# Gated delta rule in a fused three-layer kernel: decays from one product, keys turned ahead of their stages

## The chip, the cores and the metric

The kernel runs on one core of a Trainium2 chip. The metric is the device time of one execution in microseconds, lower is better. The engines are named as in the profile: PE (TensorE, matmuls and transposes; PEld is its weight load), ACT (ScalarE), DVE (VectorE), POOL (GpSimd), SP (SyncE, which starts the DMAs of the weights). Each works through its own queue in order and waits on semaphores.

## The reference

Three layers on 256 tokens of width 1024, all in fp32. The change touches the first alone, a gated convolution beside a gated delta rule with 8 heads of width 128:

```python
qkv = jax.nn.silu(causal_depthwise_conv(qkv, conv_b_w))
q, k, v = (t.reshape(bsz, s, h, GDN_HEAD_DIM) for t in jnp.split(qkv, 3, axis=-1))
q, k = l2_normalize(q), l2_normalize(k)
...
decay = jnp.exp(jnp.where(incl, gc[..., :, None] - gc[..., None, :], -jnp.inf))
kb = k * beta
low = jnp.where(strict, jnp.einsum("bhnid,bhnjd->bhnij", kb, k) * decay, 0.0)
...
attn = jnp.einsum("bhnid,bhnjd->bhnij", q, k) * decay
```

Here gc is the running sum of the gates within a chunk. So both the matrix `low` (keys against keys), which is inverted, and `attn` (queries against keys) are multiplied by the same decays, and every key is divided by its norm.

## The kernel before

**The dense work.** Weights arrive in 264 units of 512 KB. ACT rounds each to its high part `whi` (L1127), POOL subtracts it to get the low part `wlo` (L479, L480), and PE multiplies with three fast matmuls in place of one exact one (`three`, L505 to L507). Six units are in flight. A step n is one unit on PE, 24 matmuls of 128x256 in this layer. n = 0 to 31 make k, q, v and the gate z of the delta rule, a pair of heads in 8 steps (banks `gd_kq` for k and q, `gd_vz` for v and z); n = 32 to 63 make the other branch (`hcbz`, 4 steps each); then comes the out projection.

**The delta rule beside it.** Four heads are a half, and a chunk is 128 tokens, so each half has two chunks g = 0, 1. A half goes through 21 stages s. The tables `GDN_FIRST` and `GDN_BEHIND` say behind which step a stage stands: for the first half s = 0, 1, 2, 3, 4 at n = 17, 18, 19, 21, 23, then one at each n, s = 19 at 39 and s = 20 at 42; for the second half s = 0 to 4 at n = 44, 45, 46, 48, 50. Every engine runs the same loop over n, and in it does its part of the conv, the gates, the stages and the other branch in the order of the code. Each chunk has two banks of PSUM, A and B.

- Conv: ACT takes the first tap (`conv_taps`, L1205), DVE the other three (L1713), ACT the SiLU into `kT`, `qT`, `vT` (L1213). They hold head width by tokens.
- Norms: for keys ACT squares `kT` into `cv` (L1216), PE sums over the partitions with a column of ones (`k_sums_of`, L679, at n = 5, 13, 21, 29), DVE copies the four columns into `kn` (L1719) and frees the bank of k and q. Behind it `key_norms` on ACT (L1230 to L1232) takes the logarithm and two exponentials, and `gate_factors` on DVE (L1727 to L1729) multiplies them with the gates.
- Gates: at n = 8 a small projection on PE (`tail`, 24 matmuls) gives them, at n = 12 ACT and DVE work on them, at n = 14 `gate_sums_of` (L686, L687) sums them on PE, and ACT makes the exponential `gt` row 6 (L1344) at the end of n = 16.
- Stage 0: PE makes the differences of gc twice, as queries by keys in A (L748) and turned in B (L749), 16 fp32 matmuls of 128x128. ACT takes both exponentials (L1240, L1241); DVE multiplies A by the factors into `EL` (L1754) and B by the triangle `upto` into `AT` (L1755).
- Stage 1: keys against keys in A (L751), keys against queries in B (L752), and DVE multiplies both with the decays (L1758, L1759).
- Stage 2: `EL` is turned (L754). Stage 3: keys and values are turned to tokens by width (L758, L759), 16 transposes; DVE scales them into `KX` and `VB` (L1775, L1776).
- Stages 4 to 14 invert the triangle, 15 to 18 apply it, 19 gives the outputs. Stage 20 (L788) sums their squares, ACT takes Ln and Exp (L1258, L1259), DVE the product (L1827).

The other branch needs ACT for the tap `yf` (L1291) one step after a group is done and for `ya_hi` (L1296) a step later; DVE's four operations of `ya_conv` (L1852 to L1854) lie between them. On ACT the table of functions is changed by a load (L1116) where Ln and Exp follow on SiLU.

## Time and profile before

| | us |
|---|---|
| median of 3 runs | 907.57 |
| lowest and highest | 907.00, 907.66 |
| the profiled execution | 908.34 |
| its span, first to last instruction | 906.5 |
| PE busy in the span | 889.1 |
| ACT, DVE, POOL busy | 506.7, 460.1, 673.2 |

The span is one execution seen by the profiler. Busy time is the union of an engine's instructions. Matmuls overlap (one lasts 278 ns, the next starts 113 ns later), so the cost of a group on PE is the distance from the start of the first to the start of what follows, read in a timeline. Text in square brackets in a row is idle time ahead of it and what ended it. "x8" stands for eight instructions merged, and an fp32 matmul of 128x128 is two of them. In the rows of busy time by stretch stand the stretch and its length, the busy time of PE, PEld, DVE, ACT and POOL with the number of instructions, PE's granted clock (1.00 is full speed), the share of the DMA engines and GB/s.

### The profile page before, as it was taken

What the parts mean: (1) busy time and instruction counts of PE and PEld (TensorE: products, weight loads), DVE (VectorE), ACT (ScalarE), POOL (GpSimd) and SP (SyncE); (2) the same over time, 40 slices, a digit from 0 to 9 for tenths busy, and PEclk for the clock granted to TensorE, in tenths of its full rate; (3) what the DMA queues carried; (4) which work ended last, traced back from release to release, by engine and by line L of the source; (5) the groups of instructions that cost most, each with busy time, mean ns of one, the idle gap of its engine ahead of it and who ended that gap; (6) DMA issues with size and microseconds to landing.
All of it is one profiled execution on the core that took longest, in us unless ns stands there. A gap on an engine that the chain in (4) does not pass through costs nothing.

```text
span 906.5 us, 19073 instructions
## 1 busy us (share of the span) xinstructions
PE 889.1 (98%) x7549; PEld 822.0 (91%) x7549; DVE 460.1 (51%) x979; ACT 506.7 (56%) x714; POOL 673.2 (74%) x484
## 2 busy tenths in 40 slices
PE   6999999999999999999999999999999999999997
PEld 6999999999997889999999999888997899998886
DVE  4368763485531634677768777545546442220004
ACT  5775533763336456576677656565566355664331
POOL 5986766457657888857876677769796579989882
PEclk9999999999999999999999999999999999999999
DMA  8664543435444555645454554456552246666631
GB/s 314 208 222 127 162 133 125 137 101 171 138 131 176 173 182 180 192 134 163 140 152 131 153 170 143 141 194 200 176 186 93 94 155 219 206 197 208 201 116 47
DMA packets 41113, 147.14 MB, mean 162 GB/s; under 512 B 4544, under 2 KB 4672, under 8 KB 41024
## 3 DMA queue, kind: packets, MB, share of 16 engines
q1 hardware_dynamic: 39584, 141.76, 48.9%
q10 hardware_dynamic: 1440, 4.16, 1.3%
q8 instruction: 60, 0.98, 0.4%
q14 instruction: 29, 0.24, 0.1%
HBM read 144.86 MB, written 1.05 MB: 161 GB/s over the span
## 4 chain that ended last, share of the span: by engine, by line
PE 90%; DVE 3%; ACT 2%; issue 2%; POOL 2%; DMA 1%; SPq 0%; DVEq 0%; ACTq 0%; POOLq 0%
PE dense L505 26%; PE dense L507 24%; PE dense L506 24%; PE bank L866 2%; POOL wlo L480 1%; PE dense L561 1%; PE bank L703 1%; POOL wlo L479 1%; PE bank L704 1%; DVE cv L1713 1%; PE bank L898 1%; PE bank L852 1%; PE bank L1011 1%; PE bank L505 1%; PE bank L507 1%
## 5 line engine op out<-in xcount | busy, mean ns | idle before, releaser
L480 POOL TENSOR_TENSOR wlo<-raw,whi 128x512 fp32r<-128x512 f32 (+1 forms) x261 | 411.0, 1580 | 22.8 <-ACT whi L1127 22.7
L1127 ACT ACTIVATE whi<-raw 128x1024 fp32r<-128x1024 f32 (+1 forms) x264 | 275.3, 1057 | 234.7 <-PE dense L507 199.3
L479 POOL TENSOR_TENSOR wlo<-raw,whi 128x512 fp32r<-128x512 f32 x197 | 255.7, 1298 | 180.2 <-ACT whi L1127 178.2
L505 PE MATMUL dense<-x_hi,whi 128*128 128x256 f32 x1232 | 350.9, 285 | 7.4 <-DVE wlo L1644 7.4
L506 PE MATMUL dense<-x_lo,whi 128*128 128x256 f32 x1232 | 343.1, 278 | 0.0
L507 PE MATMUL dense<-x_hi,wlo 128*128 128x256 f32 x1232 | 342.9, 278 | 0.0
L505 PEld LDWEIGHTS dense<-x_hi,whi 128*128 128x128 f32 x1232 | 232.9, 189 | 11.3 <-DVE x_lo L1633 7.3
L506 PEld LDWEIGHTS dense<-x_lo,whi 128*128 128x128 f32 x1232 | 233.1, 189 | 0.7 <-issue 0.2
L507 PEld LDWEIGHTS dense<-x_hi,wlo 128*128 128x128 f32 x1232 | 233.2, 189 | 0.0
L505 PE MATMUL dense<-whi,ya_hi 128*128 128x512 f32 x192 | 77.4, 403 | 1.0 <-issue 0.8
L507 PE MATMUL dense<-whi,ya_lo 128*128 128x512 f32 x192 | 75.0, 391 | 0.0
L506 PE MATMUL dense<-wlo,ya_hi 128*128 128x512 f32 x192 | 74.9, 390 | 0.0
L1713 DVE SCALAR_TENSOR_TENSOR cv<-dense,columns,cv 128x255 f32<-128x255 f32 (+2 forms) x72 | 34.7, 482 | 24.9 <-ACT cv L1205 22.2
L505 PEld LDWEIGHTS dense<-whi,ya_hi 128*128 128x128 f32 x192 | 36.1, 188 | 9.0 <-issue 1.7
L507 PEld LDWEIGHTS dense<-whi,ya_lo 128*128 128x128 f32 x192 | 36.0, 188 | 7.9
L506 PEld LDWEIGHTS dense<-wlo,ya_hi 128*128 128x128 f32 x192 | 36.1, 188 | 7.1 <-issue 0.2
L1116 ACT ACT_TABLE_LOAD x32 | 41.1, 1283 | 1.4 <-PEq L2444 0.7
L506 PE MATMUL dense<-wlo,x_hi 128*128 128x256 f32 (+1 forms) x144 | 40.1, 279 | 0.0
L507 PE MATMUL dense<-whi,x_lo 128*128 128x256 f32 (+1 forms) x144 | 40.1, 278 | 0.0
L505 PE MATMUL dense<-whi,x_hi 128*128 128x256 f32 (+1 forms) x144 | 40.0, 278 | 0.0
L2314 DVE TENSOR_TENSOR xtok<-xtok,dense 128x512 f32<-128x512 f32 x2 | 1.4, 688 | 73.6 <-PE dense L507 73.6
L505 PE MATMUL dense<-whi,yb_hi 128*128 128x512 f32 x96 | 37.6, 392 | 0.3 <-POOL wlo L480 0.3
(334 smaller groups left out, 1386.6 us busy)
## 6 DMA issues: line engine op xcount, KB each, us to landing
raw<-weight_units_dram SPq DMA_DIRECT2D x263, 512.0 KB, 3.7
xtok<-in_x_dram SPq DMA_DIRECT2D x1, 1024.0 KB, 8.2
gb<-in_ln_g_dram ACTq DMA_DIRECT2D x2, 512.0 KB, 4.6
...
```

Of the source, the lines that this page charges most:

```text
L479: pool.tensor_tensor(wlo[:, slot, 0:half], unit_slot(u)[:, 0:half], whi[:, slot, 0:half].bitcast(F32), ALU.subtract)
L480: pool.tensor_tensor(wlo[:, slot, first:2 * half], unit_slot(u)[:, first:2 * half], whi[:, slot, first:2 * half].bitcast(F32), ALU.subtrac ...
L505: pe.matmul(out_, lh, rh, start=start, stop=False, skip_group_check=True)
L506: pe.matmul(out_, lh, rl_, start=False, stop=False, skip_group_check=True)
L507: return pe.matmul(out_, ll, rh, start=False, stop=stop, skip_group_check=True)
L561: last = pe.transpose(bank[:, j * P:(j + 1) * P], xtok[:, t, k * P:(k + 1) * P], ident)
L703: return pe.matmul(block(SB[2 * g + across], pair, side), block(LT[:, g, :], h, b), block(XN[:, g, :], h, b), start=True, stop=True)
L704: return pe.matmul(SB[2 * g + side][64 * b:64 * b + 64, pair * 32:(pair + 1) * 32], block(XN[:, g, :], 2 * pair + b, side, 256), even_odd( ...
L866: last = pe.matmul(SB[0][rows, u * P:u * P + 96], tokens_of(hk, p % 2, u // 2, u % 2)[:, rows], six, start=True, stop=True)
L1116: act.preload_act_table_set(name)
L1127: act.activation(whi[:, u % NSPL, first:], unit_slot(u)[:, first:], ACT.Copy).then_inc(hi_done, 1)
L1713: link(vec.scalar_tensor_tensor(o, bank[:, i * T:(i + 1) * T - back], colA[:, w:w + 1], o, ALU.mult, ALU.add), conv_done if back == 3 else ...
```

## The change

- Stage 0 on PE makes one product instead of two (in B). ACT takes its exponential twice, into `AT` and into B. DVE scales B into `EL` as before; the triangle is no longer applied here.
- Stage 1 makes the scores as queries against keys, so that they fit the same decays. DVE multiplies them with `AT`.
- Stage 3 turns `AT` where it had turned the keys; DVE applies the triangle `upto` to it.
- The keys are turned ahead of stage 0: `key_transposes` at n = 14 for the first half and n = 41 for the second, 8 transposes each, into the two banks A. DVE's stage 0 scales them into `KX`.
- The sums of squares: PE's 16 sums by a column of ones are gone, and ACT's Square behind each SiLU of keys with them. ACT squares the turned keys from the banks (`key_squares`, the same n as the transposes, two of 128x512), and DVE sums along the row (`key_sums`, one step later, two reductions).
- DVE frees the bank of k and q at step 5 of 8 instead of step 6.

PE behind step n = 14 (the gate sums are L686 and L687 before, L688 and L689 now; `con` holds the constants, here the identity). Before:

```order
L505 MATMUL dense<-x_hi,whi 128x256
L506 MATMUL dense<-x_lo,whi 128x256
L507 MATMUL dense<-x_hi,wlo 128x256
L686 MATMUL bank<-gt,con 128x8
L687 MATMUL bank<-gt,con 128x8
L505 MATMUL dense<-x_hi,whi 128x256
L506 MATMUL dense<-x_lo,whi 128x256
```

Now:

```order
L507 MATMUL dense<-x_lo,whi 128x256
L508 MATMUL dense<-x_hi,wlo 128x256
L688 MATMUL bank<-gt,con 128x8
L689 MATMUL bank<-gt,con 128x8
L682 MATMUL bank<-con,kT 128x128 x8
L506 MATMUL dense<-x_hi,whi 128x256
L507 MATMUL dense<-x_lo,whi 128x256
```

Eight transposes of `kT` have come between the gate sums and the next dense step; at n = 41 the same eight stand between two dense steps.

PE at stage 0 of the first half, n = 17 (`GAF` are the gates below the diagonal). Before, the start of 16 matmuls:

```order
L505 MATMUL dense<-x_hi,whi 128x256
L506 MATMUL dense<-x_lo,whi 128x256
L507 MATMUL dense<-x_hi,wlo 128x256
L748 MATMUL bank<-GAF,con 128x128
L749 MATMUL bank<-con,GAF 128x128
L748 MATMUL bank<-GAF,con 128x128
L749 MATMUL bank<-con,GAF 128x128
```

Now, all of them:

```order
L506 MATMUL dense<-x_hi,whi 128x256
L507 MATMUL dense<-x_lo,whi 128x256
L508 MATMUL dense<-x_hi,wlo 128x256
L750 MATMUL bank<-GAF,con 128x128 x8
L506 MATMUL dense<-x_hi,whi 128x256
L507 MATMUL dense<-x_lo,whi 128x256
```

The eight products with `GAF` as the weights are gone.

ACT at n = 41 and 42 (`yf` and `ya_hi` belong to the other branch, the table load and what follows to stage 20). Before:

```order
L1275 ACTIVATE dense<-dense 128x256
L1127 ACTIVATE whi<-raw 128x1024
L1291 ACTIVATE yf<-dense,columns 128x256
L1127 ACTIVATE whi<-raw 128x1024
L1296 ACTIVATE ya_hi<-dense 128x256
L1116 ACT_TABLE_LOAD
L1258 ACTIVATE bank<-bank 128x512
```

Now:

```order
L1278 ACTIVATE dense<-dense 128x256
L1128 ACTIVATE whi<-raw 128x1024
L1226 ACTIVATE LT<-bank 128x512 x2
L1294 ACTIVATE yf<-dense,columns 128x256
L1128 ACTIVATE whi<-raw 128x1024
L1299 ACTIVATE ya_hi<-dense 128x256
L1117 ACT_TABLE_LOAD
L1261 ACTIVATE bank<-bank 128x512
```

The two squares stand between the split of n = 41 and `yf`; they wait for PE's transposes of that step.

DVE there. Before:

```order
L1852 SCALAR_TENSOR_TENSOR yf<-dense,columns,yf 128x255
L1852 SCALAR_TENSOR_TENSOR yf<-dense,columns,yf 128x254
L1853 TENSOR_TENSOR yf<-dense,yf 128x256
L1854 TENSOR_TENSOR dense<-dense,yf 128x256
L1859 TENSOR_TENSOR ya_lo<-dense,ya_hi 128x256
L1827 TENSOR_TENSOR VB<-bank,KX 128x512
L1827 TENSOR_TENSOR VB<-bank,XT 128x512
```

Now:

```order
L1856 SCALAR_TENSOR_TENSOR yf<-dense,columns,yf 128x255
L1856 SCALAR_TENSOR_TENSOR yf<-dense,columns,yf 128x254
L1857 TENSOR_TENSOR yf<-dense,yf 128x256
L1858 TENSOR_TENSOR dense<-dense,yf 128x256
L1725 TENSOR_REDUCE kn<-LT 128x4 x2
L1863 TENSOR_TENSOR ya_lo<-dense,ya_hi 128x256
L1831 TENSOR_TENSOR VB<-bank,KX 128x512
L1831 TENSOR_TENSOR VB<-bank,XT 128x512
```

The two reductions stand behind the four operations of `ya_conv` and ahead of `ya_lo`.

```diff
@@ -124,6 +124,7 @@
 
 GSTEPS = 21
 GDN_FIRST = (17, 44)
+KEYS_BEHIND = (14, 41)
 GDN_BEHIND = [first + list(range(7, 20)) + [20, 22, last] for first, last in (([0, 1, 2, 4, 6], 25), ([0, 1, 2, 4, 6], 24))]
 GDN_AT = {GDN_FIRST[half] + n: (half, s) for half in range(2) for s, n in enumerate(GDN_BEHIND[half])}
 Q_SPREAD = 128.0
@@ -668,17 +669,18 @@
                     pe.wait_ge(x_ready, 1 if n == 0 else 2 * half + 2)
                 wide_unit(half, pair_of(group, p)[1 if part in ("gd_q", "gd_z") else 0], x_hi, x_lo).then_inc(split_used, 1)
 
-            def k_sums_of(p):
-
-                if p == 0:
+            def key_transposes(half):
+
+                if half == 0:
                     pe.wait_ge(rest_loaded, 16)
-                pe.wait_ge(k_squares, p + 1)
-                bank = pair_of("gd_kq", p)[0]
-                for i in range(2):
-                    for t in range(NT):
-                        last = pe.matmul(bank[:, 2 * i + t:2 * i + t + 1], cv[:, 0, i * T + t * P:i * T + (t + 1) * P], ones[:, 0:1],
-                                         start=True, stop=True)
-                last.then_inc(k_sums, 1)
+                else:
+                    pe.wait_ge(gdn_vector, dve_step(0, 19, 1))
+                    pe.wait_ge(gdn_squares, 2)
+                pe.wait_ge(conv_silu, 3 * (2 * half + 1) + 1)
+                for g in range(2):
+                    for u in range(4):
+                        last = pe.transpose(SB[2 * g][:, u * P:(u + 1) * P], kT[:, 4 * half + u, g * P:(g + 1) * P], ident)
+                    last.then_inc(k_turned, 1)
 
             def gate_sums_of():
 
@@ -745,17 +747,16 @@
                     for u, h in enumerate(heads):
                         o = slice(u * P, (u + 1) * P)
                         if s == 0:
-                            pe.matmul(A[:, o], upto, unit(GAF[:, g, :], u), start=True, stop=True)
-                            last = pe.matmul(B[:, o], unit(GAF[:, g, :], u), upto, start=True, stop=True)
+                            last = pe.matmul(B[:, o], upto, unit(GAF[:, g, :], u), start=True, stop=True)
                         elif s == 1:
                             pe.matmul(A[:, o], kT[:, h, tok], kT[:, h, tok], start=True, stop=True)
-                            last = pe.matmul(B[:, o], kT[:, h, tok], qT[:, h, tok], start=True, stop=True)
+                            last = pe.matmul(B[:, o], qT[:, h, tok], kT[:, h, tok], start=True, stop=True)
                         elif s == 2:
                             last = pe.transpose(A[:, o], unit(EL[:, g, :], u), ident)
                             if g == 1:
                                 last = pe.matmul(B[:, o], gt[:, 5, 1, h:h + 1].broadcast_to([P, P]), upto, start=True, stop=True)
                         elif s == 3:
-                            pe.transpose(A[:, o], kT[:, h, tok], ident)
+                            pe.transpose(A[:, o], unit(AT[:, g, :], u), ident)
                             last = pe.transpose(B[:, o], vT[:, h, tok], ident)
                         elif s == 14:
                             last = pe.matmul(block(A, u, 1), block(LT[:, g, :], u, 0, 256), block(XN[:, g, :], u, 0), start=True, stop=True)
@@ -814,8 +815,8 @@
                     tail_turn()
                 if n == 14:
                     gate_sums_of()
-                if n < FIRST_YA and n % 8 == 5:
-                    k_sums_of(n // 8)
+                if n in KEYS_BEHIND:
+                    key_transposes(KEYS_BEHIND.index(n))
                 if n in GDN_AT:
                     gdn(*GDN_AT[n])
             layer_tail(0)
@@ -1197,8 +1198,6 @@
                 bank = pair_of("gd_vz" if part == "v" else "gd_kq", p)[b]
                 if p == 0 and part == "k":
                     act.wait_ge(columns_loaded, 16)
-                if p > 0 and part == "k":
-                    act.wait_ge(k_sums, p)
                 for i in range(2):
                     w = 3 * 24 + GD_COLUMNS["gd_" + part] * GH + 2 * p + i
                     cols = slice(i * T, (i + 1) * T)
@@ -1212,9 +1211,6 @@
                 dst = {"k": kT, "q": qT, "v": vT}[part][:, 2 * p:2 * p + 2, :]
                 act.activation(dst, cv[:, si, :].rearrange("p (h t) -> p h t", h=2), ACT.Silu).then_inc(conv_silu, 1)
                 settle(conv_silu)
-                if part == "k":
-                    act.activation(cv[:, 0, :].rearrange("p (h t) -> p h t", h=2), dst, ACT.Square).then_inc(k_squares, 1)
-                    settle(k_squares)
 
             def gain(p):
 
@@ -1222,6 +1218,13 @@
                 act.activation(szb[:, 2 * p:2 * p + 2, :], pair_of("gd_vz", p)[1][:, :].rearrange("p (h t) -> p h t", h=2), ACT.Silu).then_inc(z_gain, 1)
                 settle(z_gain)
                 act.sem_inc(pair_free[PAIR[("gd_vz", p)]], 1)
+
+            def key_squares(half):
+
+                for g in range(2):
+                    act.wait_ge(k_turned, 2 * half + g + 1)
+                    act.activation(LT[:, g, :], SB[2 * g][:, :], ACT.Square).then_inc(k_squares, 1)
+                    settle(k_squares)
 
             def key_norms(half):
 
@@ -1237,7 +1240,7 @@
                     A, B = SB[2 * g], SB[2 * g + 1]
                     if s == 0:
                         act.wait_ge(gdn_products, pe_step(half, 0, g))
-                        link(act.activation(A[:, :], A[:, :], ACT.Exp))
+                        link(act.activation(AT[:, g, :], B[:, :], ACT.Exp))
                         act.activation(B[:, :], B[:, :], ACT.Exp).then_inc(gdn_exp, 1)
                         settle(gdn_exp)
                     if s == 2 and g == 1:
@@ -1326,6 +1329,8 @@
                     gates()
                 if n == GDN_FIRST[1]:
                     gdn(1, 0)
+                if n in KEYS_BEHIND:
+                    key_squares(KEYS_BEHIND.index(n))
                 for j in range(KT):
                     r = n - FIRST_YA - 4 * j
                     if r == 4:
@@ -1713,12 +1718,11 @@
                     link(vec.scalar_tensor_tensor(o, bank[:, i * T:(i + 1) * T - back], colA[:, w:w + 1], o, ALU.mult, ALU.add),
                          conv_done if back == 3 else vec_chain)
 
-            def take_k_sums(p):
-
-                vec.wait_ge(k_sums, p + 1)
-                link(vec.tensor_copy(kn[:, 0, :, 2 * p:2 * p + 2].rearrange("p t h -> p h t"),
-                    pair_of("gd_kq", p)[0][:, 0:4].rearrange("p (h t) -> p h t", h=2)), k_taken)
-                free("gd_kq", p)
+            def key_sums(half):
+
+                for g in range(2):
+                    vec.wait_ge(k_squares, 2 * half + g + 1)
+                    link(vec.tensor_reduce(kn[:, 0, g, 4 * half:4 * half + 4], four(LT[:, g, :]), AX_X, ALU.add), k_taken)
 
             def gate_factors(half):
 
@@ -1751,8 +1755,8 @@
                     A, B = SB[2 * g], SB[2 * g + 1]
                     if s == 0:
                         vec.wait_ge(gdn_exp, 3 * half + g + 1)
-                        link(vec.tensor_tensor(four(EL[:, g, :]), four(A[:, :]), heads(g, 8, half), ALU.mult))
-                        vec.tensor_tensor(four(AT[:, g, :]), four(B[:, :]), all4(upto), ALU.mult).then_inc(gdn_vector, 1)
+                        link(vec.tensor_tensor(four(KX[:, g, :]), four(A[:, :]), heads(g, 6 + g, half), ALU.mult))
+                        vec.tensor_tensor(four(EL[:, g, :]), four(B[:, :]), heads(g, 8, half), ALU.mult).then_inc(gdn_vector, 1)
                         settle(gdn_vector)
                     elif s == 1:
                         link(vec.scalar_tensor_tensor(EL[:, g, :], A[:, :], -1.0, EL[:, g, :], ALU.mult, ALU.mult))
@@ -1772,7 +1776,7 @@
                         link(vec.copy_predicated(blocks(XN[lower, g, :]), all64(low1, lower), four(EL[lower, g, :])[:, :, 64:P]))
                         link(vec.memset(four(XT[lower, g, :])[:, :, 0:64], 0.0))
                     elif s == 3:
-                        link(vec.tensor_tensor(four(KX[:, g, :]), four(A[:, :]), heads(g, 6 + g, half), ALU.mult))
+                        link(vec.tensor_tensor(four(AT[:, g, :]), four(A[:, :]), all4(upto), ALU.mult))
                         vec.tensor_tensor(four(VB[:, g, :]), four(B[:, :]), heads(g, 3, half), ALU.mult).then_inc(gdn_vector, 1)
                         settle(gdn_vector)
                     elif s == 15:
@@ -1878,12 +1882,14 @@
                     bounds()
                 for p in range(GH // 2):
                     r = n - 8 * p
-                    if r == 6:
-                        take_k_sums(p)
                     if 2 <= r < 8:
                         conv(p, "kqv"[(r - 2) // 2], r % 2)
+                    if r == 5:
+                        free("gd_kq", p)
                 if n == 12:
                     gates()
+                if n - 1 in KEYS_BEHIND:
+                    key_sums(KEYS_BEHIND.index(n - 1))
                 if n == GDN_FIRST[1]:
                     gate_factors(1)
                     gdn(1, 0)
```

## Rows read from the trace of the kernel before

**Rows 1.** The page: PE's busy time; shares of the ending chain.

```profile
PE 889.1 (98%) x7549; PEld 822.0 (91%) x7549; DVE 460.1 (51%) x979; ACT 506.7 (56%) x714; POOL 673.2 (74%) x484
...
PE 90%; DVE 3%; ACT 2%; issue 2%; POOL 2%; DMA 1%; SPq 0%; DVEq 0%; ACTq 0%; POOLq 0%
```

**Rows 2.** Timeline of PE, n = 5 to 7 (start, us, what, count).

```profile
23.73 0.28 PE L505 MATMUL dense<-x_hi,whi 128*128 128x256 f32 x1
...
26.33 0.28 PE L507 MATMUL dense<-x_hi,wlo 128*128 128x256 f32 x1
26.45 0.94 PE L679 MATMUL dense<-con,cv 128*128 128x1 f32 x8
27.25 0.36 PE L505 MATMUL dense<-x_hi,whi 128*128 128x256 f32 x1
27.46 0.28 PE L506 MATMUL dense<-x_lo,whi 128*128 128x256 f32 x1
...
32.99 0.28 PE L505 MATMUL dense<-x_hi,whi 128*128 128x256 f32 x1
```

**Rows 3.** Timeline of PE, stage 0 of the second half.

```profile
175.85 0.38 PE L748 MATMUL bank<-GAF,con 128*128 128x128 f32 x2
...
179.34 0.36 PE L505 MATMUL dense<-x_hi,whi 128*128 128x256 f32 x1
```

**Rows 4.** Timeline of PE, stage 3 of the second half.

```profile
198.01 0.27 PE L758 MATMUL bank<-con,kT 128*128 128x128 f32 x1
...
199.64 0.27 PE L759 MATMUL bank<-con,vT 128*128 128x128 f32 x1
```

**Rows 5.** Timeline of weight loads, start of n = 16.

```profile
59.82 0.19 PEld L505 LDWEIGHTS dense<-x_hi,whi 128*128 128x128 f32 x1 [0.26 <-DVEq L1627]
```

**Rows 6.** Timelines of ACT, PE, DVE, first half, stages 0, 1.

```profile
62.95 0.63 ACT L1213 ACTIVATE vT<-cv 128x512 f32<-128x512 f32 x1 [1.26 <-DVE cv L1713]
...
65.94 0.46 PE L748 MATMUL bank<-GAF,con 128*128 128x128 f32 x2 [0.39 <-ACT gt L1344]
...
70.23 0.69 DVE L1755 TENSOR_TENSOR AT<-bank,con 128x512 f32<-128x512 f32 x1
...
72.33 0.38 PE L751 MATMUL bank<-kT 128*128 128x128 f32 x2
```

**Rows 7.** Timeline of ACT, n = 41 and 42.

```profile
164.34 0.46 ACT L1291 ACTIVATE yf<-dense,columns 128x256 f32<-128x256 f32 x1
166.20 1.06 ACT L1127 ACTIVATE whi<-raw 128x1024 fp32r<-128x1024 f32 x1 [1.40 <-PE dense L507]
...
167.55 1.28 ACT L1116 ACT_TABLE_LOAD   x1
169.75 0.58 ACT L1258 ACTIVATE bank<-bank 128x512 f32<-128x512 f32 x1 [0.92 <-PE bank L788]
```

**Rows 8.** Timelines of DVE, n = 41, and PE, stages 1, 2.

```profile
164.90 1.00 DVE L1852 SCALAR_TENSOR_TENSOR yf<-dense,columns,yf 128x255 f32<-128x255 f32 x2 [1.53 <-ACT yf L1291]
...
166.39 0.43 DVE L1854 TENSOR_TENSOR dense<-dense,yf 128x256 f32<-128x256 f32 x1
...
182.90 0.46 PE L751 MATMUL bank<-kT 128*128 128x128 f32 x2 [0.49 <-DVE AT L1755]
...
190.96 0.33 PE L754 MATMUL bank<-con,EL 128*128 128x128 f32 x1 [0.79 <-DVE AT L1759]
```

**Rows 9.** Busy time by stretch, at start and end.

```profile
7.30:13.00 5.70, 5.64 (x26) 5.67 (x27) 3.39 (x4) 4.01 (x5) 2.71 (x3) 1.00 1.04 415
900.00:903.00 3.00, 0.53 (x5) 0.33 (x3) 2.21 (x7) 0.56 (x3) 1.45 (x2) 1.00 0.00 0
903.00:904.00 1.00, 0.00 (x0) 0.00 (x0) 0.39 (x1) 0.57 (x1) 0.00 (x0) 0.95 0.00 0
```

**Rows 10.** Groups by line and form (busy us, mean ns).

```profile
L1216 ACT ACTIVATE cv<-kT 128x512 f32<-128x512 f32 x4 | 2.5, 633 | 0.1
...
L1683 DVE TENSOR_TENSOR GAF<-con,gt 128x512 f32<-128x512 f32 x4 | 5.5, 1375 | 0.1
```

2 lines of the change are left out of this document (1 added, 1 removed).

## The prediction

> **What bounds the kernel now.** I read the page first: PE is busy almost the whole span, and the chain that ended last lies 90% on PE [rows 1]. So the time is PE's own work plus the few places where PE stands still. Removing PE work shortens the kernel only as long as nothing else decides when PE may go on. The reader then needs three things: what a matmul group really costs PE (start to start, not the duration of one, since matmuls overlap), where PE waits in the stretch that is changed, and how close ACT and DVE are behind PE there. I took the first from PE's timeline, the other two from the timelines of ACT and DVE over 50 to 200 us. Behind 200 us the program is unchanged and PE bound, so whatever has been gained by then stays. No row of that stretch shows PE waiting long for the split weights, and the change takes work off the ACT queue that feeds them.
>
> **Key sums (removed).** Dense matmuls start 0.11 us apart. Behind step n = 5 the four sums stand between starts at 26.33 and 27.25, 0.92 instead of 0.11, and the next gap is 0.21 [rows 2]: 0.91 us. The same at n = 13. At n = 21 and 29 other work of the delta rule follows directly, so the odd gap is paid anyway: 0.81 each. Together 3.44. Behind the first group the dense matmuls also come slower: 23 distances in 2.60 us (0.113) ahead of it, 47 in 5.53 (0.118) from 27.46 on [rows 2]. This lasts three steps of 24, up to the small projection at n = 8, so 0.3 more, which I take.
>
> **Bank freed earlier.** At n = 16 PE waits for gd_kq, which DVE frees only behind its copy of the sums: 0.26 on the weight load [rows 5], of which I count 0.23. DVE now frees it a step earlier. What is late next is the wlo of that step, ready long before.
>
> **Keys turned (added).** Stage 3 before issues 16 transposes, and 15 of their distances take 199.64 − 198.01 = 1.63 [rows 4], 0.109 each. Eight cost 0.87; at n = 14 they stand right behind the gate sums, at n = 41 alone, with the odd gap 0.96. Stage 3 itself keeps 16.
>
> **Stage 0 halved.** Sixteen fp32 matmuls take PE from 175.85 to 179.34 [rows 3]; eight take 1.75. Twice 1.75 is gone. Stage 1 has its operands swapped only: nothing.
>
> **Sum for PE alone:** −3.44 −0.3 −0.23 +0.87 +0.96 −3.5 = −5.6 us. This is what the change would bring if PE never waited. Now the waits.
>
> **First half (n = 12 to 18).** Stage 0 waits for the exponential of the gate sums on ACT (PE at 65.94, idle 0.39) [rows 6]. That ACT chain starts from the conv of n = 12, which comes 0.91 + 0.3 earlier, and loses the Square of the keys there, 0.63 [rows 10] with its gap of 0.03: 1.9 earlier. Its two new squares (twice 0.63, at n = 14) fall where ACT stood idle for 1.26 ahead of vT [rows 6], so they cost it nothing, without a margin. PE has saved 0.91 + 0.3 + 0.91 + 0.23 − 0.87 = 1.48 by then and arrives at 65.94 − 0.39 − 1.48 = 64.07; on ACT's account it may start at 65.94 − 1.9 = 64.04. Stage 0 thus moves by 1.9. Stage 1 needs DVE's stage 0, done at 70.92 [rows 6] and bound by ACT's exponentials, which follow in an unbroken row: also 1.9 earlier, at 69.0, and PE starts 0.14 later. PE would come at 72.33 − 1.9 − 1.75 = 68.7. So 0.5 of the 1.75 turns into a wait; stage 1 moves by about 3.1. DVE's new reductions lie behind the last conv, where DVE waits for ACT anyway. Their price no row shows. The nearest above is 1.38 for a 128x512 product with both operands in SBUF [rows 10], the nearest below 0.69 for one with an operand in a bank [rows 6]; I take 0.69, since a reduction reads one operand. At twice 1.38 they would end some 2.8 us behind the last conv (62.95 less 1.9), at 63.8, when ACT asks for them: just hidden too, and case C if not.
>
> Then 0.81 at n = 21 and 0.81 at n = 29; there DVE is loaded and PE comes closer to it, for which I give back 0.1 or nothing. Up to the end of step 41 the shift is −1.9 −1.2 −1.6 = −4.7.
>
> **Second half (n = 41 to 45), where the gain is lost.** Count from the end of dense step 41, t0 = 165.86. Before, ACT needs: whi at 166.20, after waiting 1.40 for PE; ya_hi; a table load at 167.55; and at 169.75 the Ln of stage 20 (t0 + 3.9), after 0.92 idle [rows 7]. From there ACT has no gap up to the exponentials of stage 0, and PE's stage 1 stands at 182.90, 13.15 later, where PE already waited [rows 7, 8]. So ACT, not PE, dates stage 1. Now the new squares stand in ACT's queue at n = 41 behind a wait for PE's transposes, and ahead of yf, which had run at 164.34, before t0. Queued behind that wait are yf, a whi, ya_hi, the table load and the Ln; DVE's chain waits for yf. Step by step: transposes done and seen t0 + 1.05; squares up to 1.94; yf to 2.4; DVE's four operations take 166.39 + 0.43 − 164.90 = 1.92 and start 0.1 later [rows 8], to 4.45; ya_hi with its gaps 0.45 to 4.9 (of the 1.35 between whi and the table load in [rows 7] the rest is whi); the table load 1.28 to 6.2. The Ln starts at t0 + 6.2 instead of 3.9 (its input, moved by the transposes, is there at 4.85). Stage 1 follows at 6.2 + 13.15 = t0 + 19.35; before it was at 17.04. So this half costs 2.3 instead of saving 0.8: PE waits 0.49 + 2.3 + 1.75 − 0.96, some 3.6 us (3.8 by the weight load), ahead of stage 1. The later waits of stage 2 (0.79 on its second transposes, [rows 8]) hang on the same ACT chain and stay.
>
> **Sum:** −4.7 + 2.3 = −2.4 us. The profiled execution took 908.34, with 906.5 as its span and 1.8 around it; the median of the runs is 907.57. The shift is a difference, so I take it from the median: **905.2 us**.
>
> **Rivals.** (A) *The squares are not late on ACT.* If yf and its DVE part cost less than counted, only the transposes push the Ln, by 0.96: −3.7, 903.8. For it: ACT had 1.40 + 0.92 idle there. Against: the order of the queue. (B) *PE's sum holds*: −5.6, 901.9; against it stands that PE already waits for ACT and DVE in front of both stages. (C) *More waits in the first half* (reductions at 1.38, DVE late in stages 3 to 5): 1 us more, 906.2. (D) *The clock falls.* In the stretch that is changed PE stands 0.8 us at the longest before [rows 8]; here it would stand 3.7. At the end PE works 0.53 us behind 900.00 and then stands, and the granted clock is 0.95 on average over 903 to 904, so, with 0.5 as the lower level, it fell near 903.9, some 3.4 us after PE's last work [rows 9]: about as long as the stand forecast here. At half clock the start of the program had 26 matmuls in 5.7 us, 0.22 each [rows 9]. Were it to last 5.7 again, it costs half of that, 2.85, of which 1.1 is taken from the waits ahead of stage 2: +1.75, 906.9. The Trainium skill (TensorE: Matmul & The Clock Gate, section HAM oscillation — how this bites in real kernels) warns of just this, idle gaps between bursts, after which the matmuls run at half rate; by that rule the time is that of D, and the fall at the end of the trace agrees with it. (E) *The other side:* the same fall, but the clock comes back late because PE stands again ahead of stage 2. Each us at half clock costs 0.5; to come out 0.2% slower needs 4.2 + 1.1 = 5.3 us lost, 10.6 us at half clock; two stretches of 5.7 give −2.4 − 1.1 + 5.7 = +2.2, 909.8.
>
> **How the numbers follow.** Forecast (904.3 to 906.1) 0.52; A 0.14; B 0.04; C 0.10; D 0.15; E 0.05. The range 903.0 to 907.6 leaves out B and the far side of A below, E and the dearest of D above: less than 2 in 10. A measurement of this kernel tells 0.2%, 1.8 us, from no change. Faster by more: four fifths of the forecast (0.42), A, B and some of C: 0.62. Within: the rest of the forecast, C and D, 0.32. Slower: E and a little, 0.06.
>
> **What would show it.** Right: no key sums on PE and no wait at n = 16; stage 0 at 1.75; stage 1 of the first half near 69.2; dense step 42 starting 4.7 us earlier less the transposes' 0.96; PE idle 3 to 4 us ahead of the second stage 1, released by DVE; ACT's Ln right behind the table load, not behind PE. Wrong: an idle there under 2 us (A or B), dense gaps of 0.22 after it or a granted clock under 1 (D, E), or PE waiting on stages 3 to 5 (C). The likeliest fault is a size: the unbroken ACT chain of 13.15 us.

## The result, and the profile after

The changed kernel took 907.89 us, the median of 20 runs, and the kernel before on the same chip 907.52, also 20 runs. The ratio is 1.0028, 95% interval 1.0015 to 1.0041. The ratio takes in all runs, here and in the table below. So the forecast gain of 2.4 us did not come; the kernel is slower by a little, well under 1%.

The single times say more than the median. Fourteen of the 20 lie at 907.2 to 910.1, and six at 914.1 to 916.5; the kernel before never left 906.8 to 908.6. The middle of the fourteen is 907.7, so what the ratio shows beyond 1 is nearly all due to the six, which the first batch of experiments explains. The profile is of one of the fourteen (910.06 us, span 908.2), and of the slowest: the next is 908.44. Its mean granted clock is 0.993, that of the other thirteen 0.996 or 0.997, so it shows more time at the lower clock than a common run has.

PE's work did shrink, as the page shows (PE busy 889.1 before, 886.6 now), and the ending chain has more DVE in it (3% before, now 5%), against [rows 1]:

```profile
PE 886.6 (98%) x7501; PEld 819.9 (90%) x7501; DVE 464.1 (51%) x979; ACT 507.1 (56%) x714; POOL 673.7 (74%) x484
...
PE 88%; DVE 5%; ACT 2%; issue 2%; POOL 2%; DMA 0%; DVEq 0%; SPq 0%; ACTq 0%; POOLq 0%
```

(The 886.6 has matmuls at half clock in it, see below.)

**PE's own work: as summed.** The timeline of PE behind n = 5 runs through at 0.11, where [rows 2] had the key sums; stage 0 of the second half takes 1.70 where [rows 3] had 3.49:

```profile
25.47 0.28 PE L508 MATMUL dense<-x_hi,wlo 128*128 128x256 f32 x1
25.58 0.28 PE L506 MATMUL dense<-x_hi,whi 128*128 128x256 f32 x1
25.69 0.28 PE L507 MATMUL dense<-x_lo,whi 128*128 128x256 f32 x1
...
175.06 1.95 PE L750 MATMUL bank<-GAF,con 128*128 128x128 f32 x16
176.76 0.36 PE L506 MATMUL dense<-x_hi,whi 128*128 128x256 f32 x1
```

**First half: the gain never reached stage 0.** The timelines of DVE, POOL, ACT and PE. The gate operation of DVE (L1664) starts at 49.11 instead of 51.89 (its line in the kernel before is L1659), and takes 3.35 us for 128x16 numbers:

```profile
49.11 3.35 DVE L1664 TENSOR_TENSOR gt<-gt,columns 128x16 f32<-128x16 f32 x1
52.50 0.17 DVE L1665 TENSOR_SCALAR gt<-gt 128x16 f32<-128x16 f32 x1
55.92 3.52 DVE L1688 TENSOR_TENSOR GAF<-con,gt 128x512 f32<-128x512 f32 x2
...
51.14 1.29 POOL L481 TENSOR_TENSOR wlo<-raw,whi 128x512 fp32r<-128x512 f32 x1
55.89 1.30 POOL L480 TENSOR_TENSOR wlo<-raw,whi 128x512 fp32r<-128x512 f32 x1 [3.45 <-ACT whi L1128]
57.15 1.74 POOL L481 TENSOR_TENSOR wlo<-raw,whi 128x512 fp32r<-128x512 f32 x1
...
62.58 0.63 ACT L1212 ACTIVATE vT<-cv 128x512 f32<-128x512 f32 x1 [0.98 <-DVE cv L1718]
65.24 0.18 ACT L1349 ACTIVATE gt<-bank 128x16 f32<-128x16 f32 x1
...
65.57 3.27 PE L750 MATMUL bank<-GAF,con 128*128 128x128 f32 x16 [1.87 <-ACT gt L1349]
71.80 0.38 PE L752 MATMUL bank<-kT 128*128 128x128 f32 x2
```

It ends at 52.46, just when POOL's unbroken row of subtractions ends (51.14 + 1.29), and the next operation, with POOL idle, takes 0.17. The two products GAF start with the next row of POOL and take 3.52. In the kernel before the same work took 1.92 and 2.40. The 1.92 too ended with POOL's row (52.50 + 1.28); the products, begun ahead of POOL's next row, were held less, and lengthened POOL's first subtraction to 1.71:

```profile
51.89 1.92 DVE L1659 TENSOR_TENSOR gt<-gt,columns 128x16 f32<-128x16 f32 x1
57.11 2.40 DVE L1683 TENSOR_TENSOR GAF<-con,gt 128x512 f32<-128x512 f32 x2
...
52.50 1.28 POOL L480 TENSOR_TENSOR wlo<-raw,whi 128x512 fp32r<-128x512 f32 x1
57.24 1.71 POOL L479 TENSOR_TENSOR wlo<-raw,whi 128x512 fp32r<-128x512 f32 x1 [3.46 <-ACT whi L1127]
```

So DVE's conv, ACT's `vT` (62.95 before, [rows 6]) and the exponential all moved by 0.37 and not by 1.9. PE, which had saved its part, stood 1.87 ahead of stage 0 (before: 0.39).

Even the 0.37 is not the change's. Step 2 starts 0.87 earlier in this profile than in that of before, ahead of everything that was changed (timelines of PE, after and before):

```profile
14.70 0.28 PE L506 MATMUL dense<-x_hi,whi 128*128 128x256 f32 x1
```

```profile
15.57 0.28 PE L505 MATMUL dense<-x_hi,whi 128*128 128x256 f32 x1
```

In the other profiles this step starts between 14.28 and 15.51. So a shift read between two profiles of the first half has a slack of about 1 us, and counted from step 2 stage 0 came 0.5 later.

**Second half: the chain as summed, the stand as summed.** The timeline of ACT at n = 41 and 42, against [rows 7], and PE's first matmul of stage 1, against [rows 8]:

```profile
164.62 1.23 ACT L1226 ACTIVATE LT<-bank 128x512 f32<-128x512 f32 x2 [2.07 <-PE bank L682]
165.88 0.47 ACT L1294 ACTIVATE yf<-dense,columns 128x256 f32<-128x256 f32 x1
166.39 1.06 ACT L1128 ACTIVATE whi<-raw 128x1024 fp32r<-128x1024 f32 x1
168.42 0.39 ACT L1299 ACTIVATE ya_hi<-dense 128x256 fp32r<-128x256 f32 x1 [0.97 <-DVE dense L1858]
168.83 1.28 ACT L1117 ACT_TABLE_LOAD   x1
170.12 0.58 ACT L1261 ACTIVATE bank<-bank 128x512 f32<-128x512 f32 x1
...
183.28 0.77 PE L752 MATMUL bank<-kT 128*128 128x128 f32 x2 [3.44 <-DVE EL L1759]
```

Step 41 ends at t0 = 163.98 here, so the Ln stands at t0 + 6.14 and stage 1 13.16 behind it. But t0 itself came 1.88 earlier than before (165.86), where 4.7 were forecast, and 0.87 of that is the earlier step 2.

**The clock fell twice in this run.** Rows of busy time by stretch (length, busy us and count of PE, PEld, DVE, ACT, POOL, granted clock, DMA). 0.50 is the lower of the two levels, 1.2 GHz instead of 2.4:

```profile
66.10:69.51 3.41, 3.41 (x19) 3.41 (x18) 1.25 (x4) 3.28 (x6) 2.23 (x3) 0.50 0.72 245
182.15:188.98 6.83, 5.70 (x27) 5.74 (x28) 5.13 (x10) 5.54 (x9) 3.79 (x4) 0.50 0.24 80
188.98:192.00 3.02, 3.02 (x28) 3.02 (x27) 2.64 (x5) 0.00 (x0) 2.10 (x2) 1.00 0.60 174
```

The first fall came half a us behind the stand of 1.87, the second in the stand of 3.44. From the start of stage 1 to the next dense step there are 6.28 us, where the kernel before takes 3.57.

### The profile page after: what moved, and what is told of

Same layout as the page of the kernel before. It is cut to its first block, busy times and chain, and to the rows that moved or that the text cites. A ratio compares the mean times of both kernels' runs of the same rounds, so it can differ in the third digit from the quotient of the medians.

```text
span 908.2 us, 18978 instructions
## 1 busy us (share of the span) xinstructions
PE 886.6 (98%) x7501; PEld 819.9 (90%) x7501; DVE 464.1 (51%) x979; ACT 507.1 (56%) x714; POOL 673.7 (74%) x484
## 3 DMA queue, kind: packets, MB, share of 16 engines
HBM read 144.86 MB, written 1.05 MB: 161 GB/s over the span
## 4 chain that ended last, share of the span: by engine, by line
PE 88%; DVE 5%; ACT 2%; issue 2%; POOL 2%; DMA 0%; DVEq 0%; SPq 0%; ACTq 0%; POOLq 0%
PE dense L506 25%; PE dense L508 24%; PE dense L507 24%; PE bank L867 2%; DVE cv L1718 1%; POOL wlo L481 1%; PE dense L562 1%; POOL wlo L480 1%; PE bank L705 1%; PE bank L706 1%; PE bank L752 1%; PE bank L899 1%; PE bank L853 1%; PE bank L753 1%; PE bank L1012 1%
```

## The experiments

All times are medians; "before" is the kernel before on the same chip in the same rounds. The four batches ran on different chips, and the kernel before differs by up to 0.3 us between them.

| kernel | us | lowest to highest (runs) | before | ratio, 95% interval |
|---|---|---|---|---|
| the change | 907.89 | 907.17 to 916.48 (20) | 907.52 | 1.0028 (1.0015 to 1.0041) |
| fill_both | 911.51 | 907.12 to 917.37 (12) | 907.34 | 1.0054 (1.0026 to 1.0083) |
| yf_first | 910.38 | 906.27 to 914.05 (12) | 907.34 | 1.0035 (1.0015 to 1.0055) |
| pool_pause | 906.22 | 905.23 to 916.39 (12) | 907.34 | 1.0028 (0.9995 to 1.0061) |
| old_sums | 907.00 | 906.71 to 907.61 (11) | 907.34 | 0.9998 (0.9989 to 1.0006) |
| tail_pause | 909.02 | 907.25 to 910.23 (11) | 907.20 | 1.0018 (1.0009 to 1.0027) |
| three_pauses | 906.48 | 905.23 to 907.81 (11) | 907.20 | 0.9992 (0.9984 to 1.0001) |
| best3 | 902.37 | 901.85 to 902.71 (5) | 907.20 | 0.9944 (0.9932 to 0.9957) |
| before_pauses | 907.05 | 906.60 to 907.63 (11) | 907.20 | 0.9996 (0.9987 to 1.0005) |
| yf3 | 904.49 | 903.29 to 904.97 (5) | 907.31 | 0.9959 (0.9946 to 0.9973) |
| late3 | 904.42 | 903.70 to 906.52 (7) | 907.31 | 0.9970 (0.9959 to 0.9981) |
| before_late | 905.73 | 905.37 to 906.75 (11) | 907.31 | 0.9982 (0.9973 to 0.9991) |
| fill3 | 905.20 | 904.41 to 905.98 (8) | 907.31 | 0.9973 (0.9962 to 0.9983) |
| sums3 | 905.03 | 904.68 to 905.98 (7) | 907.47 | 0.9973 (0.9963 to 0.9984) |
| decays3 | 903.86 | 903.54 to 904.34 (5) | 907.47 | 0.9958 (0.9946 to 0.9971) |
| best4 | 905.03 | 903.35 to 906.23 (11) | 907.47 | 0.9972 (0.9963 to 0.9981) |

### First batch: one suspected cause at a time

`yf_first` lets ACT do the squares of n = 14 and 41 behind its half of `ya`:

```diff
-                if n in KEYS_BEHIND:
-                    key_squares(KEYS_BEHIND.index(n))
                 for j in range(KT):
...
+                if n in KEYS_BEHIND:
+                    key_squares(KEYS_BEHIND.index(n))
```

> The changed kernel with one edit: on ACT the two squares of the keys stand behind the tap yf of the other branch at n = 41 instead of ahead of it. Theory 1 (the squares held up yf, DVE's chain and the Ln of stage 20): the Ln starts 4.9 us behind the end of dense step 41 and not 6.1, stage 1 of the second half comes 1.3 earlier, PE's stand there is 2.4 and not 3.7. Time 1.3 us below the changed kernel where the clock does the same, and more if its fall there goes too; about 1 us under the kernel before. Theory 2 (the table load or the transposes date the Ln): stand of 3.7 as before.

`pool_pause` holds POOL back while DVE does the gates and GAF:

```diff
+                if u == 16:
+                    pool.wait_ge(gates_abs, 1)
+                if u == 18:
+                    pool.wait_ge(gdn_gates, 1)
```

> The changed kernel with two waits on POOL: unit 16 of the weight splitting waits for the end of DVE's first gate operations, unit 18 for DVE's gate products; both units are needed by PE many microseconds later. Theory 1 (DVE's operations with both operands in SBUF are held up while POOL works): the first gate operation takes under 1 us and not 3.35, the gate products 1.4 for two and not 3.5; ACT's exponential of the gate sums comes about 2.5 us earlier, PE's stand ahead of stage 0 shrinks from 2.0 to under 0.5, and the fall of the clock there is gone. Time 1.5 to 2.5 us below the changed kernel. Theory 2 (they are slow for a reason of their own): durations and stand stay, time that of the changed kernel or slower by the pause.

`fill_both` puts matmuls of no use on PE where it stands, four ahead of stage 0 of the first half and seven ahead of stage 1 of the second:

```diff
+                if n == GDN_FIRST[0]:
+                    for i in range(FILL[0]):
...
+                if n == GDN_FIRST[1] + 1:
+                    for i in range(FILL[1]):
```

> The changed kernel with extra matmuls, whose results nothing reads (or which add exact zeros), put into PE's queue just ahead of the two stands: 4 of 128x256 before stage 0 of the first half, 7 on 64 rows before stage 1 of the second. No other engine's work and no order is changed. Theory 1 (the clock): the two stands of 2.0 and 3.7 us let PE's clock fall, and the time at half clock behind them is a loss of its own. Then this kernel, though it does more on PE, is faster: mean granted clock back at 0.998, stage 1 of the second half takes 3.5 us and not 6.3, time about 1 us below the kernel before, and no single run 6 us above. Theory 2 (the waits alone): the clock records mean little, the time is that of the changed kernel (within 0.5 us, and a spread up to 916).

`old_sums` keeps the new decays and turned keys, but takes the key norms as the kernel before (a Square on ACT and sums on PE at n = 5, 13, 21, 29).

> The changed kernel with the old way of the key norms: ACT's Square behind the SiLU, PE's sums by ones at n = 5, 13, 21, 29, DVE's copies, the bank freed at step 6; the new squares and reductions are out. Decays once and keys turned ahead stay. Theory 1: PE has 3.4 us more, but ACT is free of the squares at n = 14 and 41, so stage 1 of the second half stands only 2.4; sum by waits: first half -1.3, transposes +0.96, so 0.3 us under the kernel before, and at most one fall of the clock. Theory 2 (PE's sum decides): 3.7 us slower than the changed kernel, over 910.

Three of the four have medians that say little, because their runs fall into two groups 6 to 11 us apart, as those of the change do: five or six runs of twelve at 912.9 to 917.4. `old_sums` has none of these. The profiles of `yf_first` and `pool_pause` happened to be of the far group, and so show what it is. The timelines of DVE, POOL and PE in `yf_first`:

```profile
31.37 11.10 DVE L1872 TENSOR_TENSOR tail_lo<-columns,tail_hi 128x128 fp32r<-128x128 f32 x1 [0.79 <-ACT tail_hi L1322]
...
31.24 1.28 POOL L481 TENSOR_TENSOR wlo<-raw,whi 128x512 fp32r<-128x512 f32 x1
32.48 1.28 POOL L480 TENSOR_TENSOR wlo<-raw,whi 128x512 fp32r<-128x512 f32 x1
...
41.07 1.25 POOL L481 TENSOR_TENSOR wlo<-raw,whi 128x512 fp32r<-128x512 f32 x1
...
42.53 0.40 PE L506 MATMUL bank<-x_hi,tail_hi 128*16 128x256 f32 x1 [7.72 <-DVE tail_lo L1872]
```

DVE's subtraction `tail_lo`, which reads two tensors in SBUF, starts 0.13 behind the start of a POOL subtraction (also two operands in SBUF), and ends when nine of them are done and POOL's row has ended: 11.10 us. PE needs it for the small projection behind n = 8 and stands 7.72, and its clock falls in that stand. In `pool_pause` it is 11.10 and a stand of 8.32. `fill_both` has such runs too, though it fills the other two stands, so these are not their cause. In the profile of the change it had slipped in between two of POOL's, and the second of these is a little longer:

```profile
31.31 1.20 DVE L1872 TENSOR_TENSOR tail_lo<-columns,tail_hi 128x128 fp32r<-128x128 f32 x1 [0.79 <-ACT tail_hi L1322]
...
31.07 1.29 POOL L481 TENSOR_TENSOR wlo<-raw,whi 128x512 fp32r<-128x512 f32 x1
32.32 1.35 POOL L480 TENSOR_TENSOR wlo<-raw,whi 128x512 fp32r<-128x512 f32 x1
```

What the two traces show: a DVE operation with both operands in SBUF can be held out by POOL not for one instruction, but for the rest of POOL's unbroken row. The Trainium skill (SBUF — State Buffer, section Who interferes with whom) says that such a pair contends and that whoever issues first has the shared port for the whole instruction. An estimate by that sentence would be a price of one POOL instruction, at most 1.3 us here. The trace agrees that DVE waits for the end of a POOL instruction, but shows nine in a row, 11.10 us; the measurement decides.

The nearer groups can be compared: 907.2 to 908.4 (the change but for one run), 906.3 to 907.9 (`yf_first`), 905.2 to 906.5 (`pool_pause`), 907.1 to 907.8 (`fill_both`). Against what was expected:

- `pool_pause`: theory 1 holds. The gate operation takes 0.17, the two products 2.03 (1.4 had been expected), PE doesn't stand ahead of stage 0, and the middle of the nearer group is 2.2 us below that of the change.
- `yf_first`: PE's stand ahead of stage 1 is 2.1 instead of 3.4, as theory 1 has it, but the middle is only 0.2 lower, not 1.3. Why is not settled here; `yf3` takes it up.
- `fill_both`: stage 1 and its step take their old time and the clock stays at 1.00 from 12 to 903 us, but the middle is 907.5, where 1 us below the kernel before had been expected, and there are far runs: a miss. It is 2.25 us faster than the profiled run of the change, which had both falls, and 0.2 faster than the common ones.
- `old_sums`: 0.3 us under the kernel before, as expected; a stand of 2.06 and one fall of the clock. Over 910, the rival, is out.

### Second batch: pauses of POOL, and a schedule without the stand

`tail_pause` has one wait more than the change; `three_pauses` has it beside the two of `pool_pause`; `before_pauses` is the kernel before with all three.

```diff
+                if u == 10:
+                    pool.wait_ge(tail_low, 1)
```

> The kernel after, with one wait more on POOL: it begins its unit 10 only when DVE's tail_lo is done. Theory (DVE's subtraction of two SBUF operands can be held out as long as POOL runs back to back, 11.1 us in the worst case): tail_lo takes at most 1.3 us in every run, PE never stands at its tail, all runs lie at 907.0 to 908.5, none above 912, ratio to the kernel before 1.000. Rival (the runs at 914 to 916 come from something else, a DMA or the clock alone): 4 to 6 of 12 runs again at 914 to 916, whatever POOL does at unit 10. In the theory the stand of 3.4 us ahead of stage 1 of the second half and both falls of the clock stay.

> The kernel after, with three waits on POOL: unit 10 waits for tail_lo, unit 16 for the first gate operation of DVE, unit 18 for the products GAF. Theory (the same lock-out ate the 1.9 us by which stage 0 should have moved): the first gate operation takes under 1 us instead of 3.35, the two GAF products at most 2.1 us instead of 3.52, PE does not stand 2.0 us ahead of stage 0 of the first half, the clock does not fall there, and all runs lie at 905.2 to 906.5, 1.5 to 2.5 us below those with the first pause alone; ratio 0.998. Rival (the stand has another cause, ScalarE's own chain): within 0.5 us of the kernel with the first pause alone. The stand ahead of stage 1 of the second half, 3.4 us, stays in both.

> The kernel before, with the same three waits on POOL. Theory (before, the lock-out is short and mostly covered: tail_lo 1.07 us, first gate operation 1.92, GAF 2.40 for two, and PE stood only 0.39 ahead of stage 0): the gate operation under 1 us, and 0 to 0.8 us gained, 906.6 to 907.4. Rival (the pauses help by something else, such as less contention on SBUF): the same 2 us as in the changed kernel, 905.3.

`tail_pause`: no run above 910.23. The far group is gone, so the theory stands on this point; nor did any of the other eight changed kernels with this pause have a far run (70 runs with these, against 23 of 56 in the four without it). The median is 909.02, though, above the expected 907.0 to 908.5: its runs spread over 907.25 to 910.23. The profiled one (909.78) has both falls of the clock, the one at 907.25 had a higher mean clock (0.996 to 0.993). The three runs at 909.8 to 910.2 have 0.993, the three below 908 have 0.996. Why both falls come more often here than in the change isn't settled. The gate operation took 1.17 here and not 3.35, but was followed by two held for 1.21 each, and the stand ahead of stage 0 was the same 1.85.

`three_pauses`: 906.48, 2.5 us below `tail_pause`; five of its eleven runs lie above the 906.5 that had been expected as the highest. The timelines of DVE and PE:

```profile
50.00 0.17 DVE L1670 TENSOR_TENSOR gt<-gt,columns 128x16 f32<-128x16 f32 x1
55.03 2.02 DVE L1694 TENSOR_TENSOR GAF<-con,gt 128x512 f32<-128x512 f32 x2
...
63.86 1.95 PE L756 MATMUL bank<-GAF,con 128*128 128x128 f32 x16
68.86 0.46 PE L758 MATMUL bank<-kT 128*128 128x128 f32 x2 [0.22 <-DVE EL L1765]
...
180.29 0.77 PE L758 MATMUL bank<-kT 128*128 128x128 f32 x2 [3.42 <-DVE EL L1765]
```

The gate operation takes 0.17 instead of 3.35, the products 2.02 instead of 3.52. Stage 0 starts at 63.86 without a wait and stage 1 at 68.86: the prediction had 64.04 and 69.2. That they meet so well is in part luck of the start: in `before_pauses`, which lacks the change, stage 0 stands at 64.53, 1.4 earlier than before, and 1.2 of that is an earlier step 2. The stand of the second half is untouched. `before_pauses` gained 0.15 us, within the interval: in the kernel before the lock-out costs nearly nothing.

`best3` has the three pauses, the squares behind `ya`, and the second half's stages from 1 on a step later, from 19 on too:

```diff
-GDN_BEHIND = [first + list(range(7, 20)) + [20, 22, last] for first, last in (([0, 1, 2, 4, 6], 25), ([0, 1, 2, 4, 6], 24))]
+GDN_BEHIND = [first + list(range(7, 20)) + [20, 22, last] for first, last in (([0, 1, 2, 4, 6], 25),)] + [[0, 2, 3, 5, 7] + list(range(8, 21)) + [21, 23, 25]]
```

> The kernel with three pauses of POOL, and besides: ScalarE does the key squares of n=41 behind its half of ya, and stages 1 to 4 and 20 to 22 of the second half come one dense step later, with stages 5 to 19 one step later too. Theory: PE's stand of 3.4 us ahead of stage 1 shrinks to under 0.5, the clock does not fall at 182, and the time is 2 to 4 us below that with three pauses alone: 901.5 to 903.5, ratio 0.994 to 0.996, faster than both kernels. Rival (what stands ahead of stage 1 returns later, at the last stages of the second half, which now end one step later): within 0.7 us of the kernel with three pauses alone.

902.37 us: faster than both kernels, by 0.56% (0.43 to 0.68%) against before. The clock stays up over the second half's stages, and of PE's waits there only those ahead of stage 2 are left (busy time by stretch, then the timeline of PE):

```profile
170.00:200.00 30.00, 28.57 (x248) 28.14 (x248) 20.12 (x38) 22.13 (x32) 19.85 (x16) 1.00 0.37 115
```

```profile
186.59 0.66 PE L761 MATMUL bank<-con,EL 128*128 128x128 f32 x4 [0.63 <-DVE AT L1769]
188.04 0.33 PE L761 MATMUL bank<-con,EL 128*128 128x128 f32 x1 [0.80 <-DVE AT L1769]
```

### Third batch: the 4.1 us between three_pauses and best3

`yf3` is `three_pauses` with the squares behind `ya`; `late3` is `three_pauses` with the later stages; `before_late` is `before_pauses` with the later stages; `fill3` is `three_pauses` with seven matmuls of no use ahead of stage 1:

```diff
+                if n == GDN_FIRST[1] + 1:
+                    for i in range(FILL[1]):
+                        pe.matmul(pair_of("hcbz", 3)[0][0:64, 0:T], upto[64:P, 0:64], x_hi[64:P, i % KT, :].bitcast(F32), start=False, stop=False, skip_group_check=True)
```

> The kernel with three pauses of POOL, and ScalarE does the key squares of n=41 behind its half of ya instead of ahead of it; the stages stay where they were. Theory (two causes in the second half: the squares make Ln late, and the halved stage 0 brings stage 1 forward onto the chain of ScalarE and DVE): the stand ahead of stage 1 is 2.0 to 2.2 us instead of 3.4, the clock falls for 3.41 us instead of 6.83 or not at all, and the time is 1.3 to 3 us below that with three pauses alone (906.5): 903.5 to 905.2. Rival (the squares alone are the cause): the stand is gone and the time is 902.4, that of the best kernel.

> The kernel with three pauses of POOL, with stages 1 to 22 of the second half one dense step (2.72 us) later, and the key squares left ahead of ya as in the change. Theory: of the stand of 3.4 us ahead of stage 1 a step covers 2.7, so 0.7 stays, the clock does not fall at 180, and the time is 902.8 to 904.0. Rival (the order on ScalarE is the cause and the stages have nothing to do with it): over 905.

> The kernel before, with the three pauses of POOL and with stages 1 to 22 of the second half one dense step later, as in the best kernel; neither norms nor decays changed. Theory (the gain of the best kernel is the work that the change took off PE, which the stands had hidden): only its own waits of 0.79 and 0.49 us ahead of stages 3 and 2 can go, 906.0 to 907.1. Rival (the later stages alone give the gain): 903 to 904. The distance between this kernel and the best (902.4) is what the change is worth when nothing stands in its way; by the sum of PE's work in the prediction 5.6 less what had been idle.

> The kernel with three pauses of POOL, and seven matmuls of no use on PE just ahead of stage 1 of the second half, where it stands for 3.4 us (128 columns by 256, on 64 rows that hold nothing). Theory (the fallen clock is part of the price: 6.83 us at half speed, stage 1 and the step behind it took 6.28 us where they take 3.56 in the kernel before): no fall at 179 to 186, stage 1 at the same time, and 2 to 2.7 us gained, 903.8 to 904.5. Rival (the fall lies in time that PE would wait anyway): within 0.5 us of 906.5.

The first matmul of stage 1 in `yf3`, `late3` and `fill3`, one row each, and the granted clock of `fill3`:

```profile
179.33 0.46 PE L758 MATMUL bank<-kT 128*128 128x128 f32 x2 [2.07 <-DVE EL L1765]
```

```profile
180.06 0.46 PE L758 MATMUL bank<-kT 128*128 128x128 f32 x2 [0.61 <-DVE EL L1765]
```

```profile
180.29 0.46 PE L759 MATMUL bank<-kT 128*128 128x128 f32 x2 [0.27 <-DVE EL L1772]
```

```profile
170.00:200.00 30.00, 28.85 (x236) 26.86 (x235) 20.65 (x37) 21.39 (x31) 15.71 (x13) 1.00 0.30 89
```

Each of the two edits gives 2.0 (904.49, 904.42), together they give 4.1: the stand has both causes, and neither rival holds. `late3` is above the expected 904.0; its single times lie at 903.7 to 904.4 and 905.4 to 906.5, so here the profiled 903.70 is the expected case and the other was not profiled. `fill3` starts stage 1 at 180.29, to the hundredth as `three_pauses`, and is 1.3 us faster (1.4 when each is taken against the kernel before of its batch): that is the price of the fallen clock alone, less than the 2 to 2.7 expected. Part of the rest goes into a later wait: with the clock up PE waits 0.79 ahead of stage 2 again.

`before_late` gained 1.6, more than the 0.3 to 1.3 expected: the two waits of [rows 8], 0.49 + 0.79 = 1.28, are both gone, and the pauses gave 0.15. So of the 4.8 us by which `best3` beats the kernel before, 1.6 have nothing to do with the change; the change itself, with its squares behind `ya`, is worth 905.73 − 902.37 = 3.4 in a schedule that makes room for it.

### Fourth batch: 3.4 or 5.6

`sums3` takes only the decays of the change, `decays3` only the norms, each in the schedule of `best3`; the diff of `sums3` is the rest of the change undone as in `old_sums`. `best4` moves stages 2 and up a step further:

```diff
-[[0, 2, 3, 5, 7] + list(range(8, 21)) + [21, 23, 25]]
+[[0, 2, 4, 6, 8] + list(range(9, 22)) + [22, 24, 26]]
```

> Only the decays of the change (one matrix, query scores turned by transposes, keys turned ahead), the key norms as in the kernel before; three pauses of POOL and the second half's stages from 1 on one step later. Theory (the two parts add, and neither is worth its share of the sum: the halved stage 0 gives 1.4 and 1.7 us, and PE waits about 1.4 ahead of stage 2 in place of them): 904.0 to 904.6, against 905.7 for the kernel before in this schedule. Rival (the sum of PE's work holds for this part, 3.5 us): 902.2.

> Only the key norms of the change (key transposes at n=14 and 41, squares by ScalarE, sums by DVE), the decays as in the kernel before, whose stage 3 turns the keys itself; three pauses of POOL, squares behind ya, and the second half's stages from 1 on one step later. Theory (the parts add; norms are worth 3.4 less 1.6 for the transposes, units of 24 dense matmuls compared one by one): 903.6 to 904.2, against 905.7. Rival (the norms carry the whole gain): 902.4.

> The best kernel so far (902.4) with stages 2, 3 and 4 and all behind them in the second half one dense step later still. Theory (PE's waits of 0.63 and 0.80 us for AT ahead of stage 2 are idle time that a step covers): 900.8 to 901.4. Rival (the wait returns at a later stage, since the chain is as long as before): 902.0 to 902.7.

The decays alone are worth 0.7 us (905.73 to 905.03), less than either theory or rival; the norms alone 1.9 (903.86), as expected. Each of them pays for the turned keys of n = 14 and 41, some 1.6 us, which the whole change pays once. In `sums3` PE stands 0.64 + 0.79 ahead of stage 2 of the second half: with stage 0 cut by 3.7 and 1.6 added, that leaves the 0.7. The two parts would add to 0.7 + 1.9 + 1.6 = 4.2; the whole change is worth 3.4. Of the missing 0.8 the traces name 0.6 as waits (2.0 in `best3`, 1.4 in `sums3`, none above 0.25 in `decays3`).

`best4` failed, and neither expectation holds: its median is 905.03, against 900.8 to 901.4 and 902.0 to 902.7. Its runs lie at 903.3 to 903.8 (four, mean clock 0.998) and at 905.0 to 906.2 (seven, 0.995 to 0.997); only one of the four is profiled. In it stage 2 no longer waits, but PE waits at a later stage instead, in the timeline of PE:

```profile
209.32 0.45 PE L712 MATMUL bank<-EL,XN 64*64 64x32 f32 x16 [2.26 <-DVE XN L1806]
210.23 0.45 PE L712 MATMUL bank<-EL,XN 64*64 64x32 f32 x16 [0.46 <-DVE XN L1806]
```

The trace points to the lock-out once more. Ahead of the copies of `XN` four operations of `bounds`, which is no part of the delta rule, stand in DVE's queue. They took 4.5 us beside a row of POOL, and 0.7 in `best3`, where they met POOL idle. One of them, timelines of DVE in `best4` and `best3`:

```profile
204.19 1.21 DVE L1710 TENSOR_SCALAR lbc<-lbc 128x16 f32<-128x16 f32 x1
```

```profile
206.79 0.17 DVE L1710 TENSOR_SCALAR lbc<-lbc 128x16 f32<-128x16 f32 x1
```

So `best4` doesn't show what the later stages are worth; a pause of POOL there was not tried.

From the dense starts of `before_late` and `best3`, step by step, the 3.4 can be laid out. Taken off PE: key sums 1.24 + 0.81 + 1.05 + 0.84 = 3.9, stage 0 2.00 + 1.67 = 3.7. Added: transposes 0.64 + 0.98 = 1.6. That is 6.0 (the prediction: 5.6). Given back: 0.5 in the step of stage 1 of the first half, 0.5 in the step with its stages behind n = 24 (0.31 of it a wait of PE for `XN`), 1.6 ahead of stage 2 of the second half, 0.3 in the steps 50 to 52 and 0.3 at n = 1, which is of the start and not of the change; 2.8 remain in these two profiles, counted from n = 1 on. So what is missing was not mispriced on PE. It came back mostly where PE, with less to do, runs into DVE's chain: by the waits that the trace names, 1.43 ahead of stage 2, 0.31 for `XN` and 0.26 ahead of stage 1.

## Why the prediction was wrong

The forecast was 905.2, range 903.0 to 907.6; measured were 907.9 and a ratio on the other side. Step by step:

- **PE's sum, −5.6:** right in sum (−6.0 measured). Key sums with the slower spacing 3.9 against 3.74; the bank's 0.23 doesn't show in that pair of profiles, since its kernel before did not wait there either, and was never tested by itself; stage 0 of the first half −2.00, of the second −1.67, against −1.75 each; transposes at n = 41 0.98 against 0.96; those at n = 14 0.64 against 0.87.
- **The reductions:** right; two took 1.41, 0.7 each, the value taken.
- **First half, "stage 0 thus moves by 1.9":** this is the step that failed. It moved by 0.37, and not at all counted from step 2. The sum moved ACT's chain rigidly with its input and took DVE's part with it, as if the 1.92 and 2.40 of DVE's gate operation and products were their own work. All but 0.17 of the first and some 0.4 of the second was waiting for POOL, whose timeline I did not read. The gate operation started 2.78 earlier, but POOL's row ended only 1.35 earlier (52.43 against 53.78), and the products met the next row from its start: 3.52. With POOL held back in `three_pauses` they took 0.17 and 2.02, the stand ahead of stage 0 and the fall of the clock behind it were gone, and the kernel was 2.5 us faster than with the first pause alone. That shows the cause. (A smaller slip: ACT's exponentials were not an unbroken row before, they stood 0.48 for PE between the chunks.)
- **Second half, the late Ln:** right to 0.1 us: t0 + 6.14 against 6.2, stage 1 13.16 later against 13.15, a stand of 3.44 against 3.6. What the prediction did not draw from it is that the stand can be bought off: with later stages and later squares together `best3` gained 4.1 us over `three_pauses`.
- **The clock (rival D, 0.15):** the mechanism was right and should have been in the forecast, not beside it. It fell in the stand of 3.44, and also behind the one of 1.87, which no case had. Its price in the second half was put at 1.75 and is 1.3 by `fill3`. For the start of the program, taken there as half clock, the row shows a granted clock of 1.00; that the matmuls start 0.22 apart is what speaks for half.
- **Together:** `fill3` is the changed kernel with the three pauses, so without the long lock-outs, and without the fall; it took 905.20. Its distance to the kernel before is 2.1 us, or 2.0 when the 0.15 of the pauses is taken off; the forecast's was 2.4. So the two missing terms, the lock-out and the fallen clock, are nearly the whole error of the medians. In the profile they add up likewise: 2.8 short by the end of step 41, and 1.3 more lost behind it than the forecast 2.3.
- **Not foreseen at all:** the `tail_lo` of n = 7. In six of 20 runs it costs some 6 to 9 us. `tail_pause` shows the cause. That it needs the new norms to come up is shown by `old_sums`, which has the rest of the change, and the kernel before (46 runs of both in the first batch, none above 908.2). No far run of the change itself was profiled; the 11.10 is read from two of its variants.
- **Rival C (more waits in the first half, 906.2, 0.10)** named the right half, but stages 3 to 5 as its place. B and A were rightly low.
